# The last expert pass and the final norm: gate, square root table, sums and late gathers in another order

## The reference

```python
x = x + mixer(rmsnorm(x, norm1_g))
u = rmsnorm(x, norm2_g)
h = silu(einsum('btd,edf->btef', u, w_gate)) * einsum('btd,edf->btef', u, w_up)
h = h * combine[..., None]      # top-1 of 4 groups, top-2 of 4 experts in it
x = x + einsum('btef,efd->btd', h, w_down)
y = rmsnorm(x, final_norm_g)    # y * rsqrt(mean(x*x) + 1e-6) * g
```

## Time and profile before

| what | us |
|---|---|
| median of 3 timed runs | 812.83 (811.8 to 813.1) |
| the profiled execution's own time | 816.96 |
| its span, first to last instruction | 815.3 |
| TensorE busy | 782.8 (96%) |
| VectorE busy | 431.7 (53%) |
| ScalarE busy | 208.4 (26%) |
| GpSimd busy | 38.8 (5%) |

### The profile page before, as it was taken

The page is one execution under the profiler, slowest core; times in us unless marked ns, Lnnn a source line. Parts: engine busy times, 40 slices in busy tenths (PEclk is TensorE's granted clock), DMA queues, the critical chain, the costliest instruction groups (busy, mean ns, idle before and its releaser), DMA issues.

```text
span 815.3 us, 19720 instructions
## 1 busy us (share of the span) xinstructions
PE 782.8 (96%) x8426; PEld 539.0 (66%) x8426; DVE 431.7 (53%) x856; ACT 208.4 (26%) x488; POOL 38.8 (5%) x49
## 2 busy tenths in 40 slices
PE   7999999999999999999999999999999789999984
PEld 6877777787767877777777877767788533333321
DVE  5775667588768565657566455356114431111225
ACT  3122222254523312221212332220022401111134
POOL 0000000000000000000000000000000112222121
PEclk9999999999999999999999999999999889999997
DMA  9531432432212101201230102073935689999963
GB/s 341 202 113 51 137 107 71 176 105 65 91 52 80 53 28 55 68 15 61 81 104 28 51 32 80 2 266 162 384 116 207 220 326 400 390 403 393 349 224 136
DMA packets 36389, 126.89 MB, mean 156 GB/s; under 512 B 5736, under 2 KB 16008, under 8 KB 31440
## 3 DMA queue, kind: packets, MB, share of 16 engines
q1 hardware_dynamic: 32416, 115.78, 37.8%
q0 software_dynamic: 3888, 9.87, 4.3%
HBM read 106.31 MB, written 18.68 MB: 153 GB/s over the span
## 4 chain that ended last, share of the span: by engine, by line
PE 89%; DVE 4%; DMA 3%; issue 2%; ACT 1%; SPq 0%; POOL 0%; POOLq 0%; DVEq 0%; ACTq 0%
PE psum L1357 23%; PE psum L1338 12%; PE psum L1677 9%; PE psum L2554 9%; PE psum L2586 4%; PE psum L1315 4%; PE psum L1291 2%; PE psum L1302 2%; PE psum L1545 2%; PE psum L1633 1%; DVE arena L2019 1%; PE psum L1558 1%; PE psum L2534 1%; PE psum L1377 1%; PE psum L1442 1%
## 5 line engine op out<-in xcount | busy, mean ns | idle before, releaser
L2019 DVE TENSOR_TENSOR arena<-arena 128x512 f32<-128x512 f32 (+10 forms) x312 | 170.3, 546 | 50.8 <-ACT arena L1776 31.5
L1357 PE MATMUL psum<-arena 128*128 128x268 f32 x784 | 189.5, 393 | 0.0
L1357 PEld LDWEIGHTS psum<-arena 128*128 128x128 f32 x784 | 145.1, 189 | 37.8 <-issue 11.6
L1776 ACT ACTIVATE arena<-psum 128x268 f32<-128x268 f32 (+4 forms) x213 | 84.9, 406 | 282.6 <-PE psum L1357 146.6
L2019 DVE TENSOR_TENSOR arena<-psum,arena 128x256 f32<-128x256 f32 (+5 forms) x170 | 71.7, 425 | 80.9 <-PE psum L1558 21.8
L1338 PE MATMUL psum<-arena 128*128 128x268 f32 x392 | 105.0, 402 | 0.0
L1677 PE MATMUL psum<-arena 128*128 128x268 f32 x384 | 91.0, 391 | 1.6 <-DVE arena L2019 1.2
L2554 PE MATMUL psum<-arena 128*32 128x512 f32 (+1 forms) x640 | 86.2, 601 | 0.5 <-DVE arena L2707 0.3
L1338 PEld LDWEIGHTS psum<-arena 128*128 128x128 f32 x392 | 69.7, 189 | 20.4 <-issue 6.3
L1677 PEld LDWEIGHTS psum<-arena 128*128 128x128 f32 x384 | 71.1, 189 | 17.7 <-issue 3.3
L2707 DVE TENSOR_TENSOR arena<-psum,arena 128x256 f32<-128x256 f32 (+2 forms) x38 | 24.3, 663 | 104.4 <-ACT arena L2621 90.9
(11 more groups left out here) (205 smaller groups left out, 710.0 us busy)
## 6 DMA issues: line engine op xcount, KB each, us to landing
arena<-in_w_gu SPq DMA_DIRECT2D x16, 2048.0 KB, 21.6
arena<-in_w_in SPq DMA_DIRECT2D x46, 512.0 KB, 4.3
arena<-in_w_dn SPq DMA_DIRECT2D x16, 1024.0 KB, 20.6
arena<-in_w_out SPq DMA_DIRECT2D x2, 2048.0 KB, 14.6
arena<-arena SPq DMA_DIRECT2D x5, 536.0 KB, 5.2
arena<-in_x SPq DMA_DIRECT2D x8, 268.0 KB, 4.6
arena<-arena SPq DMA_DIRECT2D x16, 134.0 KB, 4.3
arena<-in_x SPq DMA_DIRECT2D x1, 2144.0 KB, 14.5
```

The source lines that it names most:

```text
L1357: last = mm(ps, w[:, k, :], x[:, k, :], start=(k == 0 and i in (0, 1, 3)), stop=(k == KD // 2 - 1), skip_group_check=i not in (0, 1, 3))
L1776: run(nc.scalar.activation(out, in_, fn, **kw), s)
L2019: run(v.tensor_tensor(out, a, b, op), s)
```

## The change

ScalarE did both first squares and roots, loaded the sigmoid table, did the gate of the last pass (11), and loaded the square root table again. It now does the first square, then the last gate, then loads the square root table once, and does the roots. VectorE does the hidden product of pass 11 ahead of the first two norms, `summed(0)` ahead of `normed(2)`, and `summed(1)` ahead of `normed(4)`. GpSimd waits for the first two readbacks before it issues the late gathers; before, it waited for them after the gathers.

```diff
--- before.py
+++ after.py
@@ -2504,13 +2504,15 @@
                                                 compute_op=ALU.add).then_inc(q_yd[e % 2], 16)
                     for q in range(2):
                         then(q_yd[q], ADDS[q], ADDS[q])
+                    then(z_x[0], 16, 16)
+                    then(z_x[1], 16, 16)
                     for j in range(LATE):
                         e = FIRST_LATE + j
                         pool.indirect_dma_start(late[:, j, :], None, x2_dram,
                                                 bass.IndirectOffsetOnAxis(ap=ids[:, e:e + 1], axis=0),
                                                 bounds_check=T - 1, oob_is_err=False).then_inc(z_in, 16)
                     then(z_in, 16 * LATE, 16 * LATE)
-                    for t in range(TT):
+                    for t in range(2, TT):
                         then(z_x[t], 16, 16)
 
                     then(z_out[0], 48, 48)
@@ -2662,26 +2664,16 @@
                         if i:
                             hidden_out(i - 1)
                             rows_out(i - 1)
-                    tables = [0]
-
-                    def table(fn):
-                        if tables[0]:
-                            at_least(act, z_sq, 3, tables[0])
-                        a(dummy, eps2[:, :], fn).then_inc(z_sq, 1)
-                        tables[0] += 1
-
                     gate(NPASS - 2)
                     hidden_out(NPASS - 3)
-                    table(ACT.Sqrt)
-                    for t in range(2):
+                    square(0)
+                    gate(NPASS - 1)
+                    hidden_out(NPASS - 2)
+                    a(dummy, eps2[:, :], ACT.Sqrt).then_inc(z_sq, 1)
+                    root(0)
+                    for t in range(1, 3):
                         square(t)
                         root(t)
-                    table(ACT.Sigmoid)
-                    gate(NPASS - 1)
-                    hidden_out(NPASS - 2)
-                    table(ACT.Sqrt)
-                    square(2)
-                    root(2)
                     hidden_out(NPASS - 1)
                     for t in range(3, TT + 2):
                         square(t)
@@ -2765,15 +2757,15 @@
                                             AX.X, ALU.add).then_inc(q_ws, 1)
                         if 0 < i < NPASS - 2:
                             rows_in(i + 1)
+                    hidden(NPASS - 1)
                     normed(0)
                     normed(1)
-                    hidden(NPASS - 1)
-                    normed(2)
                     at_least(dve, z_in, 16 * LATE, 16 * LATE)
                     summed(0)
+                    normed(2)
                     normed(3)
+                    summed(1)
                     normed(4)
-                    summed(1)
                     normed(TT)
                     for q in range(2):
                         x = late[:, LATE - 1, 512 * q:512 * q + 512]
```

## The result

The changed kernel took 817.89 us (median of 7 runs, 817.33 to 820.67) against 813.2 (7 runs, 811.8 to 816.2) for the kernel before: ratio 1.0052, interval 1.0036 to 1.0068. The forecast was 811.5, in a range of 810.0 to 813.9. The change made the kernel slower.

What follows compares the result with a forecast made beforehand. The prediction took VectorE's 12.45 us chain (797.11 to 809.56) to bound the end. Started by the gathers at 795.75, 1.36 us sooner, it gave 812.83 - 1.36 = 811.5 us, range 810.0 to 813.9.

Steps and rivals of the forecast that it cites:

- The sum's start: VectorE's last chain was to start at 795.75 instead of 797.11, 1.36 us sooner.
- my own landing of 795.7: Third late gather on GpSimd: starts at 791.0, plus 4.3 and 0.4 us, so lands at 795.7.
- The third gather's flight: Last late gather, from its start to landing: 4.3 us like the phase's first gather, plus 0.4 beside norm 0.
- break-even: Rival: lock or writes of tiles 0 and 1 hold the third gather 1 to 2 us more; 812.8, chance 0.15.
- The new gap: TensorE, ahead of the last down matmuls: down(11) waits for summed(0), 1.1 us after down(10).
- Tile 1: Its readback was to land at 787.3, with the first gather following 0.97 us behind, at 788.3.
- VectorE's chain: VectorE from summed(0) on: it was to keep its length of 12.45 us without a break.
- The tail: GpSimd's last scatters behind norm 6: the second was to start at 807.67 instead of 809.03, the tail keeping its length.
- The slower rival: Tile 1 late by itself, at 790.64; third gather lands at 799.0, 1.95 us lost, 814.8; chance 0.13.
- Fast gathers: Rival: third gather takes 3.2 us like the scatters, landing at 794.2; 2.9 us gained, 810.0; chance 0.22.
- The 3.9 us that I had it gain at root 2: ScalarE: root 2 at 793.2 against 797.1, of which 2.8 us from two removed table loads.
- the exclusive lock: Third gather's issue beside VectorE's norm 0: 0.4 us added for a partial hold, where a full block would be 0.8.

Runs made afterwards that it cites:

- lower group: Four of nine runs of the changed kernel, unchanged and timed again: 814.19 to 815.09 us; the nine together have ratio 1.0039 to the kernel before.
- upper group: Four of nine runs of the changed kernel, unchanged and timed again: 818.17 to 818.71 us; the nine together have ratio 1.0039 to the kernel before.
- the writes held: The changed kernel, with SyncE issuing the tile writes only once the late gathers have landed: ratio 1.0019 to the kernel before, 815.22 us.
- GpSimd's part undone: The changed kernel with GpSimd's two readback waits put back behind the late gathers: ratio 0.9995 to the kernel before, 813.62 us.
- ScalarE's part alone: The kernel before with only ScalarE's new order and the early hidden product, GpSimd's and VectorE's norm and sum orders as before: ratios 0.9991 and 0.9988.
- GpSimd's part alone: The kernel before with only GpSimd's two readback waits moved ahead of the late gathers: ratio 1.0036, 816.45 us.

## Why the prediction was wrong

**The sum's start was one long execution.** The step that failed first is "taken off the median, 812.83 - 1.36 = 811.5". I had noted that the profiled execution stood 4.1 us above its median, and did not ask where those 4.1 us lay. They lay in this stretch: from G to the span's end it took 34.55 us, the two later traces 30.99 and 30.79. Norm 2 started at G + 16.4 there, because tile 1 came at G + 9.9, and at 12.7 and 12.6 in the others. The later start was no property of the kernel that the change could remove. Nor was there slack to give away: the gathers, 2.1 us early in the first trace, landed at G + 14.15 and 13.8 in the later ones, where summed(0) started at 14.2 and 13.95. Such long executions are not rare (of the 17 timed runs of before beside these traces, four took 816.0 to 817.0; of the 32 beside the next kernels, none over 815.7), but the median is not made of them. With 12.7 for the start of the chain, my own landing of 795.7 (G + 14.95) would have given a loss of 2.3 us, slower, from the same terms.

**The third gather's flight was mis-sized.** The term was 4.3 + 0.4 us from its start. Measured: 7.9, 7.6 and 6.9 us in three traces of the change, 4.4 and 4.5 in two. The forecast's value is that of the good executions. In the first trace of the change the third gather started 0.55 us later than forecast (G + 10.8 and not 10.25) and flew 3.2 us longer, so it landed 3.8 us late. What the term left out was the write of tile 0, which "shares the engines": it stood among the rivals, in break-even at 1 to 2 us for the lock or the writes, and the writes alone cost 2 to 3.5. It is behind the gathers in the good executions and among them in the bad ones.

**What held.** *ScalarE:* gate 11 at 786.45, right behind its matmuls (779.29 + 7.09), one table load, root 0 done at G + 9.6 (as predicted), and roots 1 and 2 at 1.4 us each. *TensorE:* the gap went, down(10) took 3.66 us (predicted 3.65). The new gap was 5.17 us and not 1.1, and the last matmuls took 5.72, but VectorE took them up without a wait: hidden, as predicted. *Tile 1* landed at 786.54, G + 7.3 (predicted 6.6; 5.5 to 7.7 over the traces), and the first gather followed it by 0.85 us (0.97). *VectorE's chain* behind summed(0) has its 12.45 us. *The tail* is as long as it was: the second scatter starts at 809.96, G + 30.7, again 0.9 behind norm 6, although the tile writes held the first.

**The rivals.** The slower rival named the right place (VectorE waits for the gathers) and a landing close to the measured one (799.0, that is G + 18.3), but its cause was not what happened: tile 1 was not late, since the first gather went at G + 8.1 and not at 10.9. It also set its price against the long execution, so its 814.8 fell short by 3 us. Break-even had the cause, the writes, and too small a size for it; its landing of 797.9 at the latest is G + 17.15. Fast gathers did not occur: no third gather of the change flew under 4.4 us.

**The balance.** In the lower group the change starts the chain at 13.6 to 13.8 instead of 12.7, because norm 2 now stands behind summed(0): by the traces about 1 us lost, and 32.05 and 31.88 us from G to the end against 30.9. In the upper group it starts at 17.8 to 18.8: 5 to 6 us lost, 36.1 to 37.0. The measured 1.0039 is a mixture of the two; behind the 1.0052 stand seven runs of the upper group alone, the lowest at 817.33. With the writes held, the chain still starts at 15.3 and 15.7, and 1.0019 is left: that part of the loss is the later issue itself. ScalarE's new order with the early hidden product is worth a little, 0.9991, 0.9988, 0.9987 in three runs, the last with the writes held. The 3.9 us that I had it gain at root 2 were mostly the late tile 1 as well: root 2 starts at G + 12.0 in the new order (at 13.5 where tile 2 came late, in the run with GpSimd's part undone) and at 12.4 and 12.2 in the two later traces of before, where tile 1's square was over 0.2 us or less after the matmuls for gate 11. And VectorE now has norms 0 and 1 only from G + 9.6 on, since root 0 waits for gate and table; with ScalarE's part alone VectorE waits 0.2 us at most from there to the end. These kernels, some 0.1% under before, are the best that ran.

What stays open is why tile 1's readback lands at anything from G + 5.5 to 7.7 in the changed order (and once at 9.9 before): it is issued at G + 0.4 to 1.9 and flies 4.3 to 8.0 us, and no run says why. By the table, that spread decides which group an execution falls into.

## What to carry to other kernels

Before a sum is made against a profiled execution that stands several us above the median, find the stretch in which the excess lies; if it is the one that is changed, its waits are not the kernel's. A transfer that is ordered behind another to spare it contention meets whatever is issued next: list the transfers that will start in its new window, and price it with them. To put work that needs no transfer ahead of an in-order wait for one, and not behind it, looks right in these traces, where VectorE stood idle ahead of summed(0), but no timed comparison here tells its worth from noise.

## What the runs showed of the hardware

The flight of an indirect gather can jump with a small delay of its issue: issues over at 10.3 and 12.0 us landed at 13.8 and 18.7, 1.6 us of delay for 4.9. The DMA queues of the change's first trace in two stretches (q1 carries the tile writes, q0 the gathers; packets, MB, share of the 16 engines), from 793 to 794 and from 795 to 796:

```profile
q1 hardware_dynamic: 75, 0.28, 78.2%
q0 software_dynamic: 32, 0.04, 25.9%
```

```profile
q1 hardware_dynamic: 78, 0.31, 75.6%
q0 software_dynamic: 48, 0.06, 19.8%
```

In the us between them it was 0.14 MB for the writes and 0.23 for the gathers: 0.73 to 0.33 over the three. The Trainium skill (DMA: Bandwidth & Descriptors, section "Queues, rings and completion order") has each DMA engine go round its queues packet by packet, so that either queue would get its turn wherever both have work. Whether these rows agree can't be said, since they don't show how much of either queue waited at each of the 16 engines, nor where that page's packets end; that the writes are what delays the gathers was shown above by holding them.

GpSimd's issue of an indirect DMA that begins in the last 0.8 us of a norm of VectorE waits for it almost to its end, where I had priced only a part of that. The gather of GpSimd's part alone:

```profile
789.78 1.71 POOL L2511 DMA_INDIRECT arena<-x_rows,ids  x1 [0.31 <-issue]
```

It began while the norm of 789.30 to 790.59 had 0.81 us to go and took 0.69 more than the 1.02 of others. With 0.65 to go it took 1.51 (writes held, first trace), with 0.31 to go 1.17. In the earlier trace rows, 0.53 to go gave 0.39 more. Each time it is what was left less some 0.1 us. So far the trace agrees with the exclusive lock of the Trainium skill (SBUF — State Buffer, section "SBUF: two separate sides"), against the weight that the prediction gave it. The rows do not bear out the rest of that rule, by which whichever starts first holds up the other for its whole instruction. The norm of 789.11 in the change's first trace began 0.35 us into the second gather's issue, and took its usual 1.29. And in its fourth trace a gather's issue began 0.07 us into a norm; the issue took its usual 1.02, and the norm 0.04 more than usual:

```profile
790.22 1.33 DVE L2739 SCALAR_TENSOR_TENSOR arena<-arena,rs 128x1024 f32<-128x1024 f32 x1
```

```profile
790.29 1.02 POOL L2511 DMA_INDIRECT arena<-x_rows,ids  x1 [0.31 <-issue]
```
